# The second layer's input turned on VectorE and written through a scratch array, and low keys ahead of the bias rows in the first pass

## The reference

```python
for l in range(DEPTH):                                  # DEPTH = 2
    h = jnp.einsum('bsd,de->bse', x, w_in[l])
    a_v, a_gate, b_q, b_k, b_v, b_gate, c_q, c_k, c_v, c_gate = jnp.split(h, ...)
    a_out = pool_mixer(a_v, a_group_w[l], a_scale[l]) * silu(a_gate)
    b_out = swa_sink_attention(b_q, b_k, b_v, b_sinks[l]) * silu(b_gate)
    c_out = chunk_relbias_attention(c_q, c_k, c_v, c_rel_bias[l]) * silu(c_gate)
    y = jnp.einsum('bse,ed->bsd', jnp.concatenate([a_out, b_out, c_out], -1), w_out[l])
    x = layer_norm(DEEPNORM_ALPHA * x + y, ln_gain[l], ln_bias[l])
```

## Time and profile before

| | |
|---|---|
| median of 3 runs | 2852.24 us (2851.68 to 2852.72) |
| the profiled execution | 2851.78 us, its span 2849.9 us |
| TensorE busy | 2833.5 us, 99% of the span |
| VectorE, ScalarE, GpSimd busy | 60%, 46%, 44% |
| granted TensorE clock | 0.998 |
| DMA | 364.47 MB, mean 128 GB/s |
| TensorE waits for another engine | 4.3 us in all, each in the first 60 us |

### The profile page before, as it was taken

One profiled execution on the slowest core, in us unless ns is written; L12 is line 12 of the kernel. 1 busy time (PEld: TensorE's weight loads), 2 busy tenths in 40 slices (PEclk: granted clock), 3 DMA queues, 4 the chain that ended last, 5 costly groups with the idle time before them and its releaser, 6 DMA issues.

```text
span 2849.9 us, 45135 instructions
## 1 busy us (share of the span) xinstructions
PE 2833.5 (99%) x13540; PEld 2373.2 (83%) x13540; DVE 1723.5 (60%) x2898; ACT 1305.0 (46%) x2711; POOL 1248.1 (44%) x926
## 2 busy tenths in 40 slices
PE   9999999999999999999999999999999999999998
PEld 7888888888888888888888888888888888888886
DVE  5555679623766767861166666895137667678624
ACT  5444456523444445652244444664224444456521
POOL 4444444444344434444444444444444444444441
PEclk9999999999999999999999999999999999999999
DMA  6444323355444423335554443224454444322442
GB/s 202 123 124 125 93 82 84 117 169 187 130 147 144 144 86 86 84 105 165 166 169 148 150 149 93 85 82 140 145 182 139 134 144 144 88 83 81 137 156 103
DMA packets 189171, 364.47 MB, mean 128 GB/s; under 512 B 18912, under 2 KB 27136, under 8 KB 185344
## 3 DMA queue, kind: packets, MB, share of 16 engines
q1 hardware_dynamic: 185264, 347.25, 40.0%
q10 hardware_dynamic: 3792, 15.73, 1.4%
HBM read 320.94 MB, written 45.11 MB: 128 GB/s over the span
## 4 chain that ended last, share of the span: by engine, by line
PE 98%; DMA 1%; issue 0%; DVE 0%; POOL 0%; SPq 0%; ACT 0%; ACTq 0%; POOLq 0%
PE acc L557 68%; PE sc L557 17%; PE pv L557 9%; PE sc L618 2%; PE sc L655 1%; DMA bias_rows_scratch<-bias_row_scratch 1%; PE sc L581 0%; DMA first_x<-in_x_t 0%; PE acc L587 0%; PE pv L581 0%; PE sc L593 0%; PE acc L581 0%; POOL wl L1314 0%; DVE last_sums L1802 0%; DVE last_sums L1801 0%
## 5 line engine op out<-in xcount | busy, mean ns | idle before, releaser
L1314 POOL TENSOR_TENSOR wl<-raw,wh 128x512 fp32r<-128x512 f32 x920 | 1247.4, 1359 | 1558.0 <-ACT wh L928 1553.4
L928 ACT ACTIVATE wh<-raw 128x512 fp32r<-128x512 f32 x920 | 575.2, 630 | 1016.4 <-PE acc L557 691.7
L557 PE MATMUL acc<-xh,wh 128*128 128x512 f32 x2624 | 1035.4, 395 | 2.7 <-DVE xl L1347 1.9
L557 PE MATMUL acc<-xh,wl 128*128 128x512 f32 x2624 | 1023.1, 390 | 0.0
L557 PE MATMUL acc<-xl,wh 128*128 128x512 f32 x2624 | 1022.8, 390 | 0.0
L557 PEld LDWEIGHTS acc<-xh,wl 128*128 128x128 f32 x2624 | 492.5, 188 | 105.5
L557 PEld LDWEIGHTS acc<-xh,wh 128*128 128x128 f32 x2624 | 493.2, 188 | 99.1 <-DVE xl L1347 2.1
L557 PEld LDWEIGHTS acc<-xl,wh 128*128 128x128 f32 x2624 | 493.6, 188 | 93.9
L557 PE MATMUL sc<-wh,mixh 128*128 128x512 f32 x496 | 195.2, 394 | 0.1
L557 PE MATMUL sc<-wh,mixl 128*128 128x512 f32 x496 | 193.2, 390 | 0.0
L557 PE MATMUL sc<-wl,mixh 128*128 128x512 f32 x496 | 193.0, 389 | 0.0
(11 more groups left out here) (229 smaller groups left out, 3572.8 us busy)
## 6 DMA issues: line engine op xcount, KB each, us to landing
raw<-in_wall SPq DMA_DIRECT2D x920, 256.0 KB, 2.7
res_scratch<-res ACTq DMA_DIRECT2D x12, 1024.0 KB, 4.4
res<-res_scratch SPq DMA_DIRECT2D x12, 1024.0 KB, 4.9
res<-in_x SPq DMA_DIRECT2D x8, 1024.0 KB, 7.1
x_scratch<-res SPq DMA_DIRECT2D x8, 1024.0 KB, 4.7
prob<-x_scratch SPq DMA_DIRECT2D x32, 256.0 KB, 3.1
res<-x_scratch SPq DMA_DIRECT2D x8, 1024.0 KB, 5.3
hist_scratch<-mixh SPq DMA_DIRECT2D x8, 768.0 KB, 4.4
```

Of the source, the lines that this page charges most:

```text
L557: return nc.tensor.matmul(o, lhsT, rhs, start=start, stop=stop)
L928: return nc.scalar.activation(o, i, ACT.Copy, scale=scale)
L1314: nc.gpsimd.tensor_tensor(wl[:, s, :], raw[:, s, :], wh[:, s, :].bitcast(F32), ALU.subtract).then_inc(w_lo, 1)
```

## The change

In the pairs of steps 1 and 2 VectorE transposes the finished `res` in 32x32 blocks (`turn_rows`, four instructions of 128x512 per pair) into four buffers `turned`, which lie in parts of `mixh` and `mixl` that the last pair writes later. SP stores each buffer with four DMAs into a second scratch array `x1_t` (`store_turned`): 16 runs of 32 floats (128 B) per partition, 32 partitions per DMA. The block's place in DRAM completes the transpose. The stores of buffer 0 are issued in slot 21, of 1 and 2 in slot 22, of 3 in slot 23, and SP's wait for the row store moves from slot 20 to slot 23. ScalarE waits in slot 23 until the pair's 16 stores have landed. In the output stage all three steps now load x with columns on partitions and ScalarE and VectorE read it from `prob`; `transpose_x` and the waits around it are gone. In step 0 VectorE makes the low keys before the bias rows.

```diff
+        turned = [nc.alloc_sbuf_tensor_at(f"turned{n}", [P, HALF], F32, offset=x_at + 4 * HALF * (at + tile + C_PAIRS - 1))
+                  for n, (at, tile) in enumerate((a, b) for a in (2 * KT, 3 * KT) for b in (MIX_A, MIX_C))]
+        def turns(it):
+            return 1 <= it <= 2
...
# SP
-                wait_alone(ln_out, n * 16 + (64 * it + 16))
+            def store_turned(it, n, t):
+                sp.wait_ge(turned_ok, n * QT + (16 * it + t + 1))
+                for i in range(4):
+                    at = half(it) * HALF + t * P + 32 * i
+                    sp.dma_start(x1_t.rearrange("(n j a) s -> n a j s", n=4, a=32)[ds(n, 1), :, :, at:at + 32]
+                                 .rearrange("o a j b -> (o a) j b"),
+                                 turned[t][32 * i:32 * (i + 1), :].rearrange("a (j b) -> a j b", b=32)
+                                 ).then_inc(turned_out, 16)
...
+                        if s in (21, 22) and turns(it):
+                            store_turned(it - 1, p, s - 21)
+                            if s == 22:
+                                store_turned(it - 1, p, 2)
...
+                        if s == 23 and it:
+                            if turns(it):
+                                store_turned(it - 1, p, 3)
+                            wait_alone(ln_out, p * 16 + (64 * (it - 1) + 16))
...
-                            sp.wait_ge(*x_taken(it, m * 8 + gg - 1))
...
+                            sp.wait_ge(xl_ok, m * 8 + (16 * (it + 1) + gg - 1))
+                            if turns(it):
+                                sp.wait_ge(turned_out, 1024 * it + 16)
+                            src = (x_t if layer(it + 1) == 0 else x1_t).rearrange("(k p) n -> k p n", p=P)
# TensorE, output stage
-                        if n and 2 <= it + 1:
-                            pe.wait_ge(xl_ok, m * 8 + (16 * (it + 1) + 4))
-                        if n == 0 and m and 2 <= it + 1:
-                            pe.wait_ge(xl_ok, m * 8 + 16 * (it + 1))
...
-                            if u in X_AT and 2 <= it + 1:
...
-                                transpose_x(gg, (odd_banks, even_banks)[n][gg % 4])
# ScalarE, pair, after c_hi(it, p, 3)
+                    if turns(it):
+                        act.wait_ge(turned_out, p * 256 + (1024 * (it - 1) + 256 + 16))
                     mix_hi(p * 2 + (nb + 1), p + MIX_A)
# VectorE
+            def turn_rows(it, n):
+                dv.wait_ge(ln_ok, n + (4 * it + 1))
+                dv.wait_ge(turned_out, n * 256 + (1024 * it + 16))
+                for t in range(QT):
+                    V.transpose(turned[t][:], res[:, t, :]).then_inc(turned_ok, 1)
...
+                    def low_keys():
+                        dv.wait_ge(kh_ok, p + (pc + 1))
+                        keys_lo(...).then_inc(k_ok, 1)
+                    if it == 0:
+                        low_keys()
                     dv.wait_ge(bias_in, p * 16 + (16 * pc + 16))
...
                     if it:
                         gain_and_bias()
-                    dv.wait_ge(kh_ok, p + (pc + 1))
-                    keys_lo(...).then_inc(k_ok, 1)
+                        low_keys()
+                    if turns(it):
+                        turn_rows(it - 1, p)
                     queries_lo(cq, acc[1], SCALE, p * 2 + 2 * pc)
```

More of the change, by code:

```diff
@@ L120, in build @@
         x1 = nc.dram_tensor("x1_scratch", (SEQ, D), F32, kind="Internal").ap()
+        x1_t = nc.dram_tensor("x1_t_scratch", (D, SEQ), F32, kind="Internal").ap()
         res_d = nc.dram_tensor("res_scratch", (4, P, QT, 512), F32, kind="Internal").ap()
@@ L266, in build @@
         x0_in = [sem(f"x0_in{k}") for k in range(KT)]
-        tr_full = sem("tr_full")
+        turned_ok = sem("turned_ok")
+        turned_out = sem("turned_out")
         xh_ok = sem("xh_ok")
@@ L389, in _ @@
             sp.sem_inc(res_out, 16)
+            sp.sem_inc(turned_out, 16)
             def wait_alone(semaphore, value):
@@ L506, in _ @@
                             sp.wait_ge(bt_full, 2 * B_TILES * (it + 1))
-                            sp.wait_ge(*x_taken(it, m * 8 + gg - 1))
[L508 to L512, removed]
+                            sp.wait_ge(xl_ok, m * 8 + (16 * (it + 1) + gg - 1))
+                            if turns(it):
+                                sp.wait_ge(turned_out, 1024 * it + 16)
+                            src = (x_t if layer(it + 1) == 0 else x1_t).rearrange("(k p) n -> k p n", p=P)
+                            src = src[ds(m * 8 + gg, 1), :, half(it + 1) * HALF:(half(it + 1) + 1) * HALF]
                             sp.dma_start(prob[:, gg % 2, 0:512], src.rearrange("o p n -> (o p) n")
@@ L576, in project @@
                     last.then_inc(w_used, 1)
[L578 to L582, removed]
             def transpose_values(bank):
@@ L956, in x_hi_tile @@
                 copy(xh[:, ds(tile, 1), :].rearrange("p o n -> p (o n)"), source).then_inc(xh_ok, 1)
[L958 to L963, removed]
             for u in range(8):
@@ L1268, in _ @@
                             gg = X_AT.index(s)
[L1269 to L1273, removed]
+                            act.wait_ge(xin[gg % 2], m * 64 + (128 * it + 16 * (gg // 2 + 1)))
+                            x_hi_tile(m * 8 + gg, prob[:, gg % 2, 0:512])
                         if m == 0 and s < U_N:
@@ L1360, in queries_lo @@
                                            q[h][ROWS[h], :].bitcast(F32), ALU.mult, ALU.subtract).then_inc(q_ok, 1)
[L1362 to L1365, removed]
             def gate_ready(n, bank):
@@ L1582, in _ @@
                     last.then_inc(v_ok, 1)
+                    def low_keys():
+                        dv.wait_ge(kh_ok, p + (pc + 1))
+                        keys_lo([k[:, HALF:2 * HALF] for k in ck_l], acc[0], [k[:, HALF:2 * HALF] for k in ck]).then_inc(k_ok, 1)
+                    if it == 0:
+                        low_keys()
                     dv.wait_ge(bias_in, p * 16 + (16 * pc + 16))
@@ L1593, in _ @@
                         gain_and_bias()
-                    dv.wait_ge(kh_ok, p + (pc + 1))
-                    keys_lo([k[:, HALF:2 * HALF] for k in ck_l], acc[0], [k[:, HALF:2 * HALF] for k in ck]).then_inc(k_ok, 1)
+                        low_keys()
+                    if turns(it):
+                        turn_rows(it - 1, p)
                     queries_lo(cq, acc[1], SCALE, p * 2 + 2 * pc)
@@ L1726, in _ @@
                         for gg in range(4 * n, 4 * n + 4):
-                            if layer(it + 1) == 0:
-                                dv.wait_ge(xh_ok, m * 8 + (16 * (it + 1) + gg + 1))
-                                o, hi = (v[:, ds(m * 8 + gg, 1), :].rearrange("p o n -> p (o n)") for v in (xl, xh))
-                                lo(o, prob[:, gg % 2, 0:512], hi).then_inc(xl_ok, 1)
-                            else:
-                                x_lo(m * 8 + (16 * (it + 1) + gg), gg, (odd_banks, even_banks)[n][gg % 4], 2 * m + n)
+                            dv.wait_ge(xh_ok, m * 8 + (16 * (it + 1) + gg + 1))
+                            o, hi = (v[:, ds(m * 8 + gg, 1), :].rearrange("p o n -> p (o n)") for v in (xl, xh))
+                            lo(o, prob[:, gg % 2, 0:512], hi).then_inc(xl_ok, 1)
                         c = 2 * m + n
```

12 lines of the change are left out of this document (removed).

## The result

| | before | changed |
|---|---|---|
| median of 5 runs | 2852.49 us (2851.68 to 2852.94) | 2836.83 us (2836.16 to 2837.64) |
| ratio (95% interval) | | 0.9945 (0.9934 to 0.9957) |
| the profiled execution, its span | 2851.78, 2849.9 us | 2837.64, 2835.8 us |
| granted TensorE clock | 0.998 | 0.998 |

The forecast was 2835.9 us with a range of 2834.3 to 2843.0. The time came out 0.9 us above the forecast.

A forecast was written before the change was run, and what follows sets the result against it. TensorE was taken to bound the kernel, busy for 2833.5 of 2849.9 us. Terms of 15.28 and 1.07 us gave 16.35 us less with nothing added: 2835.9 us, range 2834.3 to 2843 us.

The forecast's parts named there:

- Term 1: Output stages of steps 1 and 2: without TensorE's 128 transposes each loses 7.64 us, 15.28 us together.
- Term 2: First pair of step 0: low keys ahead of the bias rows remove TensorE's wait, 1.07 us; later pairs have no gap.
- VectorE's transposes, hidden: Four per pair between low keys and low queries: 3.0 us, inside a cover of 6.1 us, so no cost.
- The block stores: DMA engines: 1 MB per pair in 8192 runs of 128 B at 17 ns each, 8.7 us per pair, landed in time.
- the rival: Slow block stores delay weight loads; 36 ns per run uses up the gain, 57 ns gives 2915 us; chance 0.09.
- SP's queue, counted at nothing: 16 DMAs per pair at 0.60 us issue, 9.6 us of SP; units 22 and 23 land in time, so no cost.
- the 0.14 rival: Small losses in the queue: unit 23 missed by 1 us in the pairs costs 4 to 8 us, 2840 to 2844 us.

The follow-up runs named there:

- experiment 4: Changed kernel with load 23 of step 2's pairs issued ahead of the two history stores; run twice: 2836.86 us and 2835.66 us.
- experiment 7: Changed kernel with eight more 128x512 transposes per pair on VectorE, behind its four, into a free buffer: 2857.52 us, ratio 1.0016.
- experiment 3: Changed kernel with SP's wait for the row store back in slot 20, ahead of load 20 and all block stores: 2844.96 us, ratio 0.9976.
- experiments 1: Kernel before with only the low keys ahead of the bias rows in step 0, x still transposed on TensorE: 2850.89 us, ratio 0.9997.
- 6 (first): Changed kernel again, unedited, for the spread; run twice: 2837.44 us, ratio 0.9947, and 2837.61 us, ratio 0.9949.
- 9: Kernel before with every group of four transposes of x on TensorE done twice into the same bank: 2866.03 us, ratio 1.0048.
- experiment 2: Changed kernel with low keys behind the bias rows in every step; run twice: 2838.97 us and 2839.43 us, both ratio 0.9953.
- 5: Changed kernel with the row store's wait back in slot 20 and load 23 of step 2's pairs ahead of the history stores: 2841.78 us, ratio 0.9963.
- experiment 8: Changed kernel with each block store issued twice, the second into another scratch array that nothing reads: 2874.40 us, ratio 1.0080.

## Why the prediction was right

**Term 1** (15.28 us): the stages' lengths give 7.63 in step 1 and 7.64 in step 2, and step 2 as a whole gives 7.62 where nothing is given back (697.01 - 689.39, experiment 4).

**Term 2** (1.07 us): the gap closes as described, with no wait at the scores behind it. It is worth 1.2 us by lengths in three of four profiles with the old order (656.13 to 656.29 us, against 654.88 to 655.02 in ten with the new). The first pair alone, from `mixl` to the first matmul behind its attention, went from 43.10 to 42.03 us: 1.07, as forecast. The other 0.1 is in the third pair (73.97, now 73.87), where the prediction had said that there was no gap to close.

**VectorE's transposes, hidden:** 0.67 us each against 0.74 from the shuffle, four in 2.49 against 3.0, in a cover of 6.1 that experiment 7 measured as 5.9 to 6.4. The Trainium skill's figure ("VectorE: DVE Perf Modes", The three transpose paths), which the prediction scaled by columns to an estimate of 1.24 us, was too high by a factor of nearly two; the row of the same shape was the better guide.

**The block stores:** 13 ns per run of 128 B against the 17 taken. The Trainium skill ("DMA: Bandwidth & Descriptors", Specifications) says that transfers under 512 B do not reach line rate, and the trace agrees: by bytes these runs cost about twice as much as large packets (13 ns against 7). It is far from the 36 ns that the rival needed, so that rival is out.

**SP's queue, counted at nothing: this is the step that was off,** and the 0.14 rival described it. Forecast: the wait taken from behind the row store only "lets load 20 leave early". Shown in experiment 3: that move is worth 6 to 6.5 us, two fifths of the change, and without it the time was 2844.96 us, 2 beyond my range. And even with it, unit 23 comes late in all four pairs of step 2 (by 3.31, 0.61, 1.86 and 0.76 us), where I had counted 1 to 3 us to spare. Two terms of the count were too small. Load 23 was to leave 10.7 us behind the row store (1535.8, 1546.5) and left 12.3 to 13.4 behind it (13.36 in the first pair: 1452.76, 1466.12); SP needed 3.69 us for buffer 0's four stores, not 4 * 0.60 = 2.4. And it was to land 3.1 us after its issue plus an allowance for the history, where the trace of the kernel before already had 5.7 to 6.3 us for this very load; the 3.1 was the median of the pieces of x.

Against this, I had let TensorE feel a late ScalarE from about 1.5 us on. Unit 23 up to 1.99 us late cost at most 0.3 us; 2.9 to 3.3 us late cost 1.0 to 1.45. That is why one pair out of eight loses, where the rival spoke of all. It is luck that two errors, a margin that was not there and a tolerance larger than counted, nearly cancelled: the forecast of no loss at all is wrong in mechanism and only 1 to 1.45 us off.

**The profiled execution,** 2837.64 against 2835.4 forecast, is 2.2 off: 1.45 from that pair, 1.40 from step 3, less 0.36 at the start, 0.13 in term 2 and 0.13 outside the span.

**Step 3 stays open.** In the changed kernel ScalarE waits 6.69 us for a load at 2124.00, where before it was 5.19 at 2137.76, and TensorE waits once:

```profile
2124.00 0.63 ACT L925 ACTIVATE wh<-raw 128x512 fp32r<-128x512 f32 x1 [6.69 <-DMA raw<-in_wall]
...
2130.71 0.50 PE L574 MATMUL acc<-xh,wh 128*128 128x512 f32 x1 [1.10 <-POOL wl L1303]
```

The orders of instructions are the same there. Step 3 has 717.2 us in the profiles of before and of experiments 1, 3, 4 (first), 6 (first), 7 and 9, and 0.5 to 2.0 more in the others: after, experiment 2 twice, 4 (second), 5, 6 (second) and 8. All that have it read the new array in the output stage, but so do four that have it not. One difference can be read in SP's queue ahead of the late loads: the first load into `prob` behind `res` in step 3 (`in_ln_gain`) landed 6.6 to 7.7 us behind its issue in the seven profiles with the excess, 4.9 to 5.3 in six of the seven without, and 6.7 in the other one (experiment 4, first, 717.26 us). Everything behind it in the queue is late with it. Why it is slow in some executions is not shown. No experiment was aimed at it, and whether the change makes it likelier or it is chance can't be told from 14 profiles of one execution each.

## What to carry to other kernels

When a change puts many DMAs on the queue that also prefetches, write down for each prefetch the time from issue to due, with everything ahead of it in the queue: the issue times and the bytes. Take the landing time from the same load in the trace you have, behind the same stores, and not from the median of all. A wait in that queue that costs nothing today is a term of the sum as soon as the queue is full: here moving it was worth two fifths of the gain. And where one engine bounds, measure each stage from one fixed instruction to another: step 1 repeated to 0.05 us in the profiles without a loss in it, where medians scatter by 1.

## What the runs showed of the hardware

- A transpose of 128x512 float32 in 32x32 blocks took VectorE 0.67 us, less than the shuffle of the same shape (0.74).
- 64 KB written to DRAM in 512 runs of 128 B landed in 2.5 us (median of 128), and a run took an engine about 13 ns, some twice the 7 ns that 128 B of a large packet cost. The small reads of the earlier trace rows had given 17.
- SP issued such stores 0.53 us apart in the undisturbed stretch (eight in 4.26 us), some held up to 2.09 us. In experiment 8 the 24 of a pair stood 0.65 us apart on average, one load among them.
- A load of 256 KB issued right behind two stores of 768 KB landed 5.6 to 7.7 us after its issue, against a median of 2.7; in the kernel before, without block stores, 5.7 to 6.3.
- ScalarE 3.31 us late with the split of unit 23 cost TensorE 1.45 us, and up to 1.99 us late at most 0.3. In experiment 8 it was 7.63 us late with unit 22, and TensorE waited 3.97 us.
- Behind such waits the granted clock was at 0.50 (1.2 GHz) for a stretch: in two of eight pairs of experiment 7, behind waits of 1.53 and 0.28 us, and in all four pairs of step 2 of experiment 8, behind 3.4 to 4.2 us. One such stretch cost 1.55 us. In experiment 3 a wait of 1.90 us was followed by none.
